# A reordered attention stage and unread 128x256 products in a two-layer streaming encoder

## The reference

```python
u = h @ w_in                                   # split among four groups
A: (window mean over 2/4/8/16 tokens - token) @ w_grp * scale        # "pool"
B: S = S*w - (S kk)(kk*a) + v k ; y = S r ; groupnorm, gate          # "rule": RWKV-7 delta rule
C: b * conv3(c * x_in)                                               # "conv"
D: A[t,s] = sigmoid(z_ts) * prod_{s<j<t} (1 - sigmoid(z_tj)), s < t  # stick-breaking attention
   y = A @ v            # prompt: 512 keys; sample: 128 cached keys + the new ones
x += post2(concat(A, B, C, D) @ w_out)
```

## Time and profile before

| | us |
|---|---|
| median of 3 runs | 2754.32 (2751.14 to 2754.84) |
| the profiled execution | 2749.94 |
| its span, first to last instruction | 2748.1 |
| PE busy in the span | 2651.9 |

### The profile page before, as it was taken

How to read it: one execution, slowest core, us unless ns; L and a number is a source line. 1 busy time by engine, 2 the same in 40 slices (tenths; PEclk the granted TensorE clock), 3 DMA queues, 4 the chain that set the end, 5 groups by cost and what they waited for, 6 DMA issues and landing times.

```text
span 2748.1 us, 48430 instructions
## 1 busy us (share of the span) xinstructions
PE 2651.9 (96%) x20994; PEld 2593.6 (94%) x20994; DVE 992.9 (36%) x1483; ACT 753.6 (27%) x1074; POOL 902.4 (33%) x444
## 2 busy tenths in 40 slices
PE   8999999998889999999999999999988899999998
PEld 8999999997779999999999999998977799999998
DVE  6222201876554522210252221038655554222102
ACT  4222211423322422221232222133143143222211
POOL 5333332533112533333353333334321044333331
PEclk9999999999889999999999999999997999999999
DMA  4222222323002222222222222222220022222221
GB/s 118 75 70 76 73 72 64 91 62 112 10 3 71 62 76 69 76 72 78 73 64 75 76 73 75 72 81 68 67 92 10 2 70 77 76 76 69 76 73 67
DMA packets 356052, 188.38 MB, mean 69 GB/s; under 512 B 16330, under 2 KB 354086, under 8 KB 355912
## 3 DMA queue, kind: packets, MB, share of 16 engines
q1 hardware_dynamic: 355668, 186.25, 23.1%
q10 hardware_dynamic: 244, 0.08, 0.0%
HBM read 179.50 MB, written 6.80 MB: 68 GB/s over the span
## 4 chain that ended last, share of the span: by engine, by line
PE 88%; DVE 6%; DVEq 2%; ACT 1%; issue 1%; DMA 1%; ACTq 0%; SPq 0%; POOL 0%
PE ps L1504 25%; PE ps L1506 25%; PE ps L1505 25%; PE ps L1550 3%; PE ps L1498 1%; DVE xT L1009 1%; PE ps L2011 1%; PE ps L1995 1%; PE ps L2007 1%; DVE ps L1005 1%; DVE h_split L1029 1%; PE ps L1700 1%; DMA w_raw<-in_ffn_w_gate 1%; PE ps L1523 0%; PE ps L1940 0%
## 5 line engine op out<-in xcount | busy, mean ns | idle before, releaser
L553 POOL TENSOR_TENSOR w_lo<-w_raw,w_hi 128x1024 fp32r<-128x1024 f32 (+1 forms) x330 | 781.2, 2369 | 1663.6 <-ACT w_hi L618 1662.6
L1504 PE MATMUL ps<-h_split,w_hi 128*128 128x384 f32 (+1 forms) x3520 | 1103.9, 314 | 10.4 <-DVEq L1484 5.0
L1506 PE MATMUL ps<-h_split,w_lo 128*128 128x384 f32 (+1 forms) x3520 | 1093.3, 311 | 0.0
L1505 PE MATMUL ps<-h_split,w_hi 128*128 128x384 f32 (+1 forms) x3520 | 1083.1, 308 | 0.0
L1504 PEld LDWEIGHTS ps<-h_split,w_hi 128*128 128x128 f32 x3520 | 661.5, 188 | 17.4 <-DVEq L1484 5.4
L1506 PEld LDWEIGHTS ps<-h_split,w_lo 128*128 128x128 f32 x3520 | 667.9, 190 | 0.0
L1505 PEld LDWEIGHTS ps<-h_split,w_hi 128*128 128x128 f32 x3520 | 663.3, 188 | 0.4
L618 ACT ACTIVATE w_hi<-w_raw 128x1024 fp32r<-128x1024 f32 (+1 forms) x330 | 342.2, 1038 | 797.6 <-DMA w_raw<-in_ffn_w_down 363.8
L1504 PE MATMUL ps<-hidden_split,w_hi 128*128 128x384 f32 (+1 forms) x1344 | 419.6, 312 | 0.0
L1506 PE MATMUL ps<-hidden_split,w_lo 128*128 128x384 f32 (+1 forms) x1344 | 416.6, 310 | 0.0
L1091 DVE TENSOR_TENSOR scratch<-ps,square_sums 128x640 f32<-128x640 f32 x176 | 144.4, 824 | 753.0 <-PE ps L1506 750.7
(11 more groups left out here) (315 smaller groups left out, 2020.8 us busy)
## 6 DMA issues: line engine op xcount, KB each, us to landing
w_raw<-in_ffn_w_gate SPq DMA_DIRECT2D x88, 512.0 KB, 3.7
w_raw<-in_ffn_w_up SPq DMA_DIRECT2D x88, 512.0 KB, 3.7
w_raw<-in_ffn_w_down SPq DMA_DIRECT2D x64, 448.0 KB, 3.2
w_raw<-in_w_in SPq DMA_DIRECT2D x42, 512.0 KB, 3.8
w_raw<-in_ffn_w_down SPq DMA_DIRECT2D x32, 512.0 KB, 3.5
w_raw<-in_w_out SPq DMA_DIRECT2D x16, 512.0 KB, 3.5
token_rows<-in_x_prompt SPq DMA_DIRECT2D x4, 512.0 KB, 5.2
k_cache<-in_cache_sb_k SPq DMA_DIRECT2D x2, 1024.0 KB, 5.7
```

Source lines behind the costliest of these rows:

```text
L553: nc.gpsimd.tensor_tensor(WLO[s][:, 0:n], RAW[s][:, 0:n], WHI[s][:, 0:n].bitcast(F32), ALU.subtract).then_inc(sem(f"lo_ready{s}"), 1)
L1504: MM(out, hi, mov[:, 0, cols], start=first, stop=False)
L1505: MM(out, hi, mov[:, 1, cols], start=False, stop=False)
L1506: return MM(out, lo, mov[:, 0, cols], start=False, stop=last)
```

## The change

- The sample units come before query block 0: the last units are now the two small ones. Unit 8 uses the same PSUM banks as units 7 and 9, so `scores` of units 8 and 9 wait for the sigmoids of the unit just before.
- The high copies of conv and pool move from ahead of unit 0 to behind unit 7's sigmoids on ACT; their low parts move from POOL to DVE, behind unit 7's multiply. `k_cacheT` moves to other memory, and `fill_out` no longer waits for `lo_split`.
- ACT loads the sigmoid table early, by a one-column activation after the key copy; the rounding of output block 2 moves from there to unit 7's place.
- The prompt's attention output is split in two pieces: query blocks 2 and 3 (`attn_late_hi`), copied out behind unit 9's sigmoids, and blocks 0 and 1 at the end. One semaphore, `attn_split`, covers all three subtractions, and the rule's first product waits for it.
- `exps(0)` moves ahead of unit 9's copy, `operands(0)` ahead of the subtractions, and the ten transposes of the rule's values ahead of unit 7's value products.
- `busy(bank, n)`: n products of the identity with 256 columns of constants, into a bank that is overwritten later without being read: one in each of `scores(4)` to `scores(9)`, four after the last unit, four after each of the rule's first two `scores`; 18 per layer.

```diff
-UNIT_LIST = [(i, g) for ii in ((PT - 1, PT - 2),) for g in range(GC) for i in ii] + [(i, g) for i in (1, 0, PT) for g in range(GC)]
+UNIT_LIST = [(i, g) for ii in ((PT - 1, PT - 2),) for g in range(GC) for i in ii] + [(i, g) for i in (1, PT, 0) for g in range(GC)]
+SAMPLE_AT = UNIT_LIST.index((PT, 0))
...
-            return 6 if u == 1 else 2 * ((u + 1) % 2)
+            return 6 if u == 1 else 0 if u == UNITS - 2 else 2 * ((u + 1) % 2)
...
# POOL
-                pool.wait_ge(sem("conv_hi"), nth(l, "conv_hi"))
-                nc.gpsimd.tensor_tensor(H[:, 4:6, 1, :], CV[:, 4:6, :], H[:, 4:6, 0, :].bitcast(F32), ALU.subtract)
-                pool.wait_ge(sem("pool_hi"), nth(l, "pool_hi"))
-                nc.gpsimd.tensor_tensor(H[:, 0:2, 1, :], CV[:, 2:4, :], H[:, 0:2, 0, :].bitcast(F32), ALU.subtract)
-                pool.drain().then_inc(sem("lo_split"), 1)
...
# ACT
-                    round_weights(in_block(l) + t + 3)
+                    if t < NW - 1:
+                        round_weights(in_block(l) + t + 3)
...
+                        A(HCOLS[:, 0:1], EPSC[:, 0:1], ACT.Sigmoid)
...
-                    act.wait_ge(sem("lo_split"), l + 1)
...
-                A(H[:, 4:6, 0, :], CV[:, 4:6, :], ACT.Copy).then_inc(sem("conv_hi"), 1)
-                A(H[:, 0:2, 0, :], CV[:, 2:4, :], ACT.Copy).then_inc(sem("pool_hi"), 1)
...
+                    if it == PAST_AT + GC - 1:
+                        A(H[:, 4:6, 0, :], CV[:, 4:6, :], ACT.Copy).then_inc(sem("conv_hi"), 1)
+                        A(H[:, 0:2, 0, :], CV[:, 2:4, :], ACT.Copy).then_inc(sem("pool_hi"), 1)
+                    if it == UNITS - 3:
+                        act.wait_ge(sem("attn_done"), l * UNITS + 2 * GC)
+                        A(attn_rows(1, 0), PROMPT_OUT[1], ACT.Copy).then_inc(sem("attn_late_hi"), 1)
+                        round_weights(in_block(l) + NW + 2)
                     if it == UNITS - 2:
-                        act.wait_ge(sem("attn_done"), l * UNITS + PT * GC)
-                        A(H[:, 6:8, 0, 0:TP].rearrange("p g (i n) -> p g i n", n=P), PROMPT_OUT, ACT.Copy).then_inc(sem("attn_hi"), 1)
+                        exps(0)
...
                 A(H[:, 6:8, 0, TP:T], SAMPLE_OUT, ACT.Copy).then_inc(sem("attn_sample_hi"), 1)
+                A(attn_rows(0, 0), PROMPT_OUT[0], ACT.Copy).then_inc(sem("attn_hi"), 1)
...
# DVE, in the loop over units and behind it
+                    if u == UNITS - 3:
+                        dve.wait_ge(sem("conv_hi"), nth(l, "conv_hi"))
+                        V.tensor_tensor(H[:, 4:6, 1, :], CV[:, 4:6, :], H[:, 4:6, 0, :].bitcast(F32), ALU.subtract)
+                        dve.wait_ge(sem("pool_hi"), nth(l, "pool_hi"))
+                        V.tensor_tensor(H[:, 0:2, 1, :], CV[:, 2:4, :], H[:, 0:2, 0, :].bitcast(F32), ALU.subtract)
+                        fence().then_inc(sem("lo_split"), 1)
...
+                operands(0)
+                dve.wait_ge(sem("attn_late_hi"), nth(l, "attn_late_hi"))
+                V.tensor_tensor(attn_rows(1, 1), PROMPT_OUT[1], attn_rows(1, 0).bitcast(F32), ALU.subtract)
                 dve.wait_ge(sem("attn_done"), (l + 1) * UNITS)
...
-                operands(0)
                 dve.wait_ge(sem("attn_sample_hi"), nth(l, "attn_sample_hi"))
                 V.tensor_tensor(H[:, 6:8, 1, TP:T], SAMPLE_OUT, H[:, 6:8, 0, TP:T].bitcast(F32), ALU.subtract)
+                dve.wait_ge(sem("attn_hi"), nth(l, "attn_hi"))
+                V.tensor_tensor(attn_rows(0, 1), PROMPT_OUT[0], attn_rows(0, 0).bitcast(F32), ALU.subtract)
+                fence().then_inc(sem("attn_split"), 1)
...
# PE
+            def busy(bank, n):
+                for _ in range(n):
+                    MM(PS[:, bank, 0:2 * P], IDENT, CONS[:, 0:2 * P], start=True, stop=True, skip_group_check=True)
...
-                        pe.wait_ge(sem("sig_ready"), l * UNITS + u - 1)
+                        pe.wait_ge(sem("sig_ready"), l * UNITS + (u if u >= UNITS - 2 else u - 1))
...
+                    if u >= 4:
+                        busy(z, 1)
...
+                    if it == UNITS - 2:
+                        pe.wait_ge(sem("sig_ready"), (l + 1) * UNITS)
+                        for i in range(TT):
+                            for g in range(GC):
+                                at = (i * GC + g) * P
+                                end = turn(PSF[:, at:at + P], XS[:, 4 + g, i * P:(i + 1) * P])
+                        end.then_inc(sem("values_turned"), 1)
...
+                busy(4, 4)
                 pe.wait_ge(sem("attn_split"), nth(l, "attn_split"))
...
+                    if p == 0:
+                        pe.wait_ge(sem("values_out"), nth(l, "values_out"))
+                        busy(1, 4)
```

More of the change, by code:

```diff
@@ L208, in build @@
         Y = sb("y", [P, DC, T], stack=scope)
+        scope.close()
+        scope = ExitStack()
+        KCT = sb("k_cacheT", [P, GC, NSTR, PAST], stack=scope)
         scope.close()
@@ L276, in build @@
         XTR = sb("invT", [P, 4, NH, CH], stack=scope)
-        ARS = [sb(f"alpha_rho{p}", [P, GC, 2, len(PAIRS[p]) * P], stack=scope) for p in range(3)]
+        ARS = [sb(f"alpha_rho{p}", [P, GC, 2, len(PAIRS[p]) * P], stack=scope) for p in (1, 2)]
         TOK = sb("beta_kappa_rows", [P, 4, 2, G], stack=scope)
-        BK = sb("beta_kappa", [P, 2, GC, 2 * P], stack=scope)
         RH = sb("rhs", [P, G], stack=scope)
@@ L364, in build @@
         GCOLS = [COLS[:, 0:3], COLS[:, 3:5]]
-        PROMPT_OUT = PSF[:, 6 * 512:8 * 512].rearrange("p (i g n) -> p g i n", i=PT, g=GC)
+        PROMPT_OUT = [PS[:, 6 + k, :].rearrange("p (i g n) -> p g i n", i=2, g=GC) for k in range(2)]
         SAMPLE_OUT = PS[:, 3, 0:GC * P].rearrange("p (g n) -> p g n", g=GC)
@@ L837, in fill_out, with exps @@
                     act.wait_ge(sem("fill_turned"), l * FILLS + k + 1)
-                    act.wait_ge(sem("lo_split"), l + 1)
                     b = k * 4 % NSTR
                     A(KCT[:, k // 2, b:b + 4, :].rearrange("p b n -> p (b n)"), PS[:, 6, :], ACT.Copy).then_inc(sem("fill_out"), 1)
+                def exps(p):
+                    if p:
+                        act.wait_ge(sem("operands"), l * len(PAIRS) + p)
+                    else:
+                        act.wait_ge(sem("kv_stored"), (l + 1) * 4 * 16)
+                    w = len(PAIRS[p]) * P
+                    ts = slice(p * 2 * P, p * 2 * P + w)
+                    A(EXPS[:, 0, :, 0:w], CS[:, :, ts], ACT.Exp, scale=-DECAY)
+                    A(EXPS[:, 1, :, 0:w], CS[:, :, ts], ACT.Exp, scale=DECAY)
+                    A(EXPS[:, 2, :, 0:w], CSP[:, :, ts], ACT.Exp, scale=-DECAY)
+                    act.drain().then_inc(sem("exps_ready"), 1)
                 keep_sig(0)
@@ L849, in _ @@
                         g = it - PAST_AT
-                        z = z_bank(PT * GC + g)
+                        z = z_bank(SAMPLE_AT + g)
                         act.wait_ge(sem("past_scores"), l * GC + g + 1)
@@ L1356, in operands @@
                     fence().then_inc(sem("operands"), 1)
-                dve.wait_ge(sem("attn_hi"), nth(l, "attn_hi"))
-                V.tensor_tensor(H[:, 6:8, 1, 0:TP].rearrange("p g (i n) -> p g i n", n=P), PROMPT_OUT,
-                                H[:, 6:8, 0, 0:TP].bitcast(F32).rearrange("p g (i n) -> p g i n", n=P), ALU.subtract)
-                fence().then_inc(sem("attn_split"), 1)
+                for u in range(UNITS):
+                    i, s = unit(u)[0], u % 2
+                    n = P * (i + 1) if i < PT else 2 * P
+                    dve.wait_ge(sem("sig_ready"), l * UNITS + u + 1)
+                    if u == 1:
+                        u_evac(NW - 1)
+                    for e in range(2):
+                        ke = KE[:, s, e, n - 1::-1]
+                        V.tensor_tensor_scan(ke, ke, ke, 1.0, ALU.mult, ALU.bypass)
+                    fence()
+                    sig = SIG[:, s, :, 0:n - 1]
+                    V.tensor_tensor(sig, sig, KE[:, s, :, 1:n], ALU.mult)
+                    fence().then_inc(sem("attn_ready"), 1)
+                    if u == UNITS - 3:
[7 more added lines that the diff above has]
+                V.tensor_tensor(attn_rows(1, 1), PROMPT_OUT[1], attn_rows(1, 0).bitcast(F32), ALU.subtract)
                 dve.wait_ge(sem("attn_done"), (l + 1) * UNITS)
@@ L1904, in heads @@
                         yield h, h // 2, h % 2, slice(h * HD, (h + 1) * HD), slice(64 * (h % 2), 64 * (h % 2) + 64)
-                for i in range(TT):
-                    for g in range(GC):
-                        at = (i * GC + g) * P
-                        end = turn(PSF[:, at:at + P], XS[:, 4 + g, i * P:(i + 1) * P])
-                end.then_inc(sem("values_turned"), 1)
+                busy(4, 4)
                 pe.wait_ge(sem("attn_split"), nth(l, "attn_split"))
```

38 lines of the change are left out of this document (8 added, 30 removed).

## The result

The changed kernel takes 2728.35 us in the median (2725.60 to 2732.62, 4 runs) against 2752.73 for the kernel before on the same chip (2750.22 to 2754.84, 4 runs): a ratio of 0.9914, 95% interval 0.9899 to 0.993. That is 24.4 us less between the medians, or 23.7 by the ratio. The forecast was 13.2 less (2741) and its range ended at 2733. The direction was right, the size was not.

The account below looks back on a forecast made before the run. PE, busy 2651.9 of 2748.1 us, bounds the kernel; only its waits and half clock can be won. Full-clock terms sum to -17.6, plus 4.4 for clock falls: -13.2, so 2754.3 becomes 2741, range 2733 to 2750.

Parts of the forecast that it names:

- to unit 1's transposes: Projection's end to unit 1's transposes: 0.89 us wait gone, scans 5.12 us less, 0.2 given back; -5.8 / -5.8 us.
- to the first past-key products: Unit 1's transposes to the first past-key products: full clock, two unread products and a 0.7 us wait added; -2.7 / -0.8 us.
- to the rule's first transposes: Past-key products to the rule's first transposes: unread products and new waits make it 28.5 us; +4.4 / +1.0 us.
- first two score steps: The rule's first two score steps: at full clock, unread products fitting into DVE's mask wait; -2.6 / -1.3 us.
- first round: The rule's first inversion round: 3.03 us at full clock, from 5.14 and 4.88; -2.1 / -1.9 us.
- POOL's lock: Unit 1's scans on DVE: with POOL's subtractions moved away, the pair falls from 6.93 to 1.81 us.
- The moved work of DVE and ACT: Past-key products to rule: DVE's moved subtractions and ACT's copies cause new waits of 0.7, 1.5, 0.8 and 2.3 us.
- The narrow value products hardly depend on the clock: Units with narrow products: 32 records take 1.84 us at half clock, past-key products 1.96 at full; no clock gain counted.
- I take one such fall per layer: Around the sample value products: one clock fall per layer, mended by the four unread products; +2.2 us per layer, chance 0.55.
- full clock throughout: Rival for the whole stretch: unread products keep the clock at 1.00 to the end; -17.6 us, 2737, chance 0.20.
- The rest of the kernel ... only moves: Outside the stretch: FFN and projections stay at full clock and only shift in time; no gain or loss counted.
- POOL's moved low part: Output block 2, 2.35 us: ends about 1.2 us before DVE's operand builds, costing nothing; rival of collision 2746, chance 0.07.

Follow-up runs that it names:

- more in the rule: Changed kernel plus unread products in three waits of the later rule (6 of 128x256, 48 and 32 of 64x64): 2728.08 us, ratio 0.9926.
- before three times: The kernel before, unedited, in its first profile and two more: 2749.94, 2744.41 and 2748.52 us profiled.
- order alone: Changed kernel without any unread products, with the order, moved subtractions and early table kept: 2738.74 us, ratio 0.9956.
- singles only: Changed kernel without the three groups of four unread products, keeping the six single ones ahead of the scores of units 4 to 9: 2739.98 us, ratio 0.9969.
- unread products alone: The kernel before plus the same 18 unread products per layer at the same places, without the reordering: 2741.96 us, ratio 0.9978.
- old order: Changed kernel with the sample units last again, their score banks and waits as before, everything else kept: 2732.54 us, ratio 0.9941.
- groups only: Changed kernel without the six single unread products ahead of the scores of units 4 to 9, keeping the three groups of four: 2729.99 us, ratio 0.9936.
- shorter in the rule: As "more in the rule", with 24 instead of 48 and 16 instead of 32 products of 64x64: 2720.07 us, ratio 0.9889.
- no POOL subtractions: The kernel before with POOL's two subtractions (low parts of conv and pool) left out, nothing else changed: 2739.36 us, ratio 0.9955.
- second profile after: Profile of the changed kernel run again, with no edit, beside the kernel before: 2728.16 us, ratio 0.9918.
- the last kernel: As "shorter in the rule", without the six single unread products ahead of the scores of units 4 to 9: 2719.18 us, ratio 0.9889.

## Why the prediction fell short

The terms, in the prediction's marks (layer 0 / layer 1, us in the profile after):

| step | after, forecast | after, measured |
|---|---|---|
| to unit 1's transposes | 3.9 | 3.93 / 3.93 |
| to the first past-key products | 10.1 | 10.45 / 10.45 |
| to the rule's first transposes | 28.5 | 30.88 / 27.39 |
| first two score steps | 8.5 | 8.14 / 8.15 |
| first round | 3.03 | 3.59 / 3.60 |

- *POOL's lock*: right, to 0.1 us, and shown by the run without POOL's subtractions.
- *The moved work of DVE and ACT*: right in the sum, within 1.1 us in layer 1 (27.39 by 28.5). Waits of 0.62 and 1.17 us stand before the scores of units 8 and 9, and 1.20 ahead of the rule in layer 0 (forecast 0.7, 1.5 and 2.3). Only unit 9's values wait longer for their copy behind `exps(0)`, 2.00 instead of 0.8, and in layer 1 the fall followed that wait.
- *"The narrow value products hardly depend on the clock"*: wrong. The forecast compared them at half clock with other products at full clock. The same 32 records take 1.84 at half and 1.06 at full, so the two sets of a layer gain 1.6 us for which the forecast has nothing. In layer 1 this outweighs the longer wait of unit 9's values.
- *The unread products*: 1.99 for four, less the tail of 0.15 that the forecast used, is 0.46 each by its 0.43.
- *The first round*: 0.6 too short. The forecast took a later round; the first has a wait of 0.53 for DVE's masks in it.
- *"I take one such fall per layer", +2.2 each*: failed. Of the four layers in the two profiles after, one (layer 0, 56.99) has a long fall, 3.4 us over the best (53.5), and one (54.83) two short ones, 1.3 over it. The four average 54.7, so falls cost 1.2 per layer. The long one, 16.3 us at 0.50, is over the 12 us that the prediction itself gave as a sign of being wrong. Measured against the same profile of before, the stretches gain 15.3 and 17.4 us, which is the rival of full clock throughout (-17.6, 2737) more than the forecast. That rival had a chance of 0.20.
- *"The rest of the kernel ... only moves"*: failed. The rest of the rule has falls of its own, which the prediction had as luck in the range's lower end and not as something that the change shifts. In the profiles of all kernels but "more in the rule" that part goes with its clock: about 78.3 us at 1.00, 79.8 at 0.98, 81.4 at 0.96, 84.5 at 0.92, 85.2 at 0.90, 86.4 at 0.88. As an estimate from these, a microsecond of half clock costs 0.4 to 0.5 us there (86.4 at 0.88 is 8.1 us more, for 20.7 us of half clock). Five profiles without the groups of four ahead of the rule (before three times, order alone, singles only) have 2618.4 to 2625.1 us outside the stretch, mean 2622.5; five with them and nothing else in the rule (after twice, unread products alone, old order, groups only) 2616.8 to 2620.7, mean 2618.5. That is about 4 us, though the run without POOL's subtractions, at 2619.6 without groups, overlaps, and the changed kernel's own two profiles show only 1.1 of it (2620.5 in the mean, by 2621.6 for the three of before). The shorter products in the rule make the point by themselves: filling three waits took the rest of the rule from 79.8 to 85.2 us down to 78.3 (79.8 in one layer of four).
- *POOL's moved low part*: right. It ran from 710.79 to 713.15 in layer 0, and the operand builds began at 714.33, the 1.2 us margin of the forecast. How near it was, the old unit order shows, where it met a multiply.

Of the 11.2 us that the gain went beyond the forecast (24.4 less 13.2), the first pair of profiles shows 2.1 in the stretch and 2.0 in the rest. The other 7.1 are scatter between runs, which one profile of each kernel could not show: 2.8 us by which the profiled run of before lay below its median, and 4.3 by which that of after lay above. So "a measured median should move by the same amount" as the profiled run failed too. The scatter goes with the clock: over 101 runs a microsecond more of half clock than the kernel's own mean goes with 0.28 us more time (correlation 0.89). As an estimate from that slope, the 61 us less half clock of after are 17 us; the other 4 to 7 are idle time that the order took out, less what the unread products cost. Order alone divides the other way: 3 us of clock, 7 to 9 of idle time. This is no more than an estimate, since half clock had a different price in different places. Without it, the runs show that both halves of the change count: 12.1 us for the order and 6.0 for the unread products, 18.1 in sum, where both at once gave 22.5 (each of these by the ratio, good to about 4 us).

Still open: why the falls come in some executions and not in others of the same kernel. Also, "order alone" and "no POOL subtractions" end equal in time while their stretches differ by 4.2 us in sum; the rest of the span, 3.1 longer in the first, hides it, and with one profile of each that difference was not settled.

## What to carry to other kernels

Price a wait twice: by its own length and by the half clock that may follow it. A few unread products that just fit into a wait, measured by the duration of their records, bought 8 us here; twice as many, about 2 us too long at two of the three places, gave all of it back. And half clock has no fixed price: among the attention's small units 14 us of it per layer cost no more in one kernel than the products that prevent it, while in the rule's rounds and chains each cost 0.4 to 0.5 us, so place the filling ahead of those.

## What the runs showed of the hardware

The clock fell in two ways. In layer 1 of after, the rule's falls went with waits of 3.07, 2.97 and 1.91 us. Once these were filled, five of six layers stayed at 1.00 (0.90 and 1.00 in the windows above); the sixth had one fall behind the wait of 1.67, which all six have. The Trainium skill, "TensorE: Matmul & The Clock Gate", section "HAM oscillation — how this bites in real kernels", tells of DMA waits of about 3 to 5 us between dense stretches, each of which brings the clock down. The rule's rows agree in kind, not in size or regularity: falls went with shorter waits here, and in the second profile after, waits of 2.97 and 1.91 us passed without one. In the attention of the last kernel the granted clock was 0.54 over 15.00 us in which PE was busy for 14.74, on the small units' products and transposes. In the 10 us ahead of it PE's longest wait was 0.49 us, before the second run of the narrow past-key products. So a long wait is not what stands ahead of this fall, and no run here tells what brings it.

Half clock and time parted: "more in the rule" and "shorter in the rule" have the same 36 to 37 us of it and differ by 8 us, of which 7.4 lie in the rule, where the longer products outlast their waits (82.0 by 78.3 in both layers), and the last kernel has 56 and is no slower than the one with 37, with six products per layer fewer.
